# Memory cross-attention of a two-layer decoder trunk: queries made transposed in two half blocks, heads taken in pairs

## The chip, the core and the metric

The kernel runs on one core of a Trainium2 chip. The metric is the device time of one launch in microseconds (us), as a median of several runs. Six engines appear below: PE (TensorE) multiplies matrices into the accumulation memory PSUM, DVE (VectorE) and ACT (ScalarE) do elementwise work, POOL (GpSimd) here does one elementwise job only, SP (SyncE) issues the transfers of the weights. Each engine runs its own instructions in the order in which the code issues them, and waits on semaphores for the others.

## What is computed

Two layers, each with three sub-layers that add to the rows `x` (256 tokens, 1024 columns). The change is in the second sub-layer:

```
def memory_xattn(h, mem_h, wq, wk, wv, q_norm, k_norm, wo):
    q = rms_norm((h @ wq).reshape(B, S, XA_HEADS, XA_HEAD_DIM), q_norm)
    k = rms_norm((mem_h @ wk).reshape(B, M, XA_HEADS, XA_HEAD_DIM), k_norm)
    v = (mem_h @ wv).reshape(B, M, XA_HEADS, XA_HEAD_DIM)
    s = jnp.einsum('bshd,bmhd->bhsm', q, k).astype(jnp.float32) * (XA_HEAD_DIM ** -0.5)
    p = jax.nn.softmax(s, axis=-1)
    o = jnp.einsum('bhsm,bmhd->bshd', p.astype(v.dtype), v).reshape(B, S, XA_WIDTH)
    return o @ wo
...
x = x + merged @ w_out[l]
x = x + memory_xattn(rms_norm(x, xa_norm[l]), rms_norm(mem, mem_norm[l]), ...)
x = x + peer_ffn(rms_norm(x, ffn_norm[l]), ...)
```

There are 4 heads of 128, 256 tokens and 256 memory rows. `rms_norm` divides a row by the root of its mean square. Around this sub-layer stand the output projection of the first one (`w_out`) and the expert network, which takes most of the time and is not touched.

## The kernel before

**Weights come as a stream of pieces.** A piece is 128 x 512 numbers of some weight matrix. The table `ORDER` lists the pieces of a layer: the blocks out0, out1 (`w_out`), xq (8 pieces of `wq`), xo0, xo1 (4 pieces each of `wo`, by halves of the output columns), pq0, pq1 (8 each, queries of the expert network), and before and behind them other blocks. For each piece ACT rounds it to a high part (`hi`, L495), POOL subtracts that to get the low part (L464), and PE multiplies with both. There are four slots for pieces, so ACT and POOL work on a piece only when PE is done with the piece four places ahead of it (semaphore `used`). On PE, `take(n)` (L853) takes the next n pieces. A normal piece is six matmuls with 512 moving columns (L874 to L876): the activations are held stationary and the weights move. A piece of pq0 or pq1 (`query_piece`, L843) is twelve matmuls with 256 moving columns (L848 to L850): here the weights are stationary, and the result comes out transposed.

**Order of the work.** There is no scheduler: each engine's order is the order of the code. PE around the change is at L1036 to L1100, ACT at L644 to L696, DVE at L1573 to L1646. `rows_T` transposes rows through PE; `hi_T` on ACT and `lo_T` on DVE then make the high and low parts of the transposed rows that the next pieces multiply. `a.step` and `d.step` make ACT and DVE wait for each of their own instructions before the next.

**The attention.** PE takes all 8 xq pieces, the last 6 of them in one go (L1039). DVE scales the queries by the rows' norm (L1589), ACT squares them (L659), DVE sums the squares (L1593), PE transposes the queries (L1045, recorded at L824), ACT copies them with the gain (L662), ACT takes the root (L551) and switches its function table to exp (L665). Then come four units, each of one 128-token half and one pair of heads: scores on PE (`xscores`, L1051), maximum on DVE (L1605, L1606), exp on ACT with the sum on the side (L669), transposition of the probabilities on PE (`xprobs`, recorded at L824), copy on DVE (L1611), values on PE (`xvalues`, L1068). At the end of each token half DVE divides by the sums (L1621, L1623), PE transposes the result (L1088), `hi_T` and `lo_T` split it, and PE goes on with `take(6)` (L1092): the four pieces of xo0 and the first two of xo1. Then it waits until DVE has added xo0 to X (`add_block`, L1571), transposes the first half of X (L1096), and takes four more pieces.

No piece of the weight stream is multiplied between the last xq piece and the first xo piece.

## Time and profile before

| | us |
|---|---|
| median of 3 runs | 2165.35 (2164.05 to 2165.48) |
| the profiled execution | 2163.49 |
| its span, first to last instruction | 2161.7 |
| PE busy / POOL busy / DVE busy / ACT busy | 2124.3 / 1716.0 / 1244.7 / 1191.0 |

The profiled execution is 1.86 us below the median of the runs; 1.79 us of it lie outside the span. The granted TensorE clock is full over the whole span. Times in the trace are microseconds from the first instruction. The two layers are the same code in a loop: what stands at 259 us in the first layer stands again at 1330 us in the second, with gaps of the same length, so the text reads the first layer and doubles.

### The profile page before, as it was taken

The page shows a single profiled execution, that of the slowest core. Times are in us where ns is not written, and L with a number is a line of the kernel's source. Part 1 is how long each engine was busy: PE and PEld are TensorE (multiplying, and loading weights), DVE is VectorE, ACT ScalarE, POOL GpSimd, SP SyncE. Part 2 cuts the span into 40 slices and gives each one's busy share as a digit, 9 for nine tenths or more (in the row PEclk, how much of TensorE's full clock was granted, in tenths as well). Part 3 has the DMA queues.
Part 4 walks back from the last instruction along what each step waited for, and adds up shares of the span by engine and source line. Part 5 has one row for each costly group of instructions (what it writes and reads, how often), then busy time and mean ns, then how long its engine had stood idle before and what let it go on. Part 6 is the DMA issues. An engine that isn't in the chain of part 4 may idle for free.

```text
span 2161.7 us, 50003 instructions
## 1 busy us (share of the span) xinstructions
PE 2124.3 (98%) x14654; PEld 1832.6 (85%) x14654; DVE 1244.7 (58%) x2401; ACT 1191.0 (55%) x2285; POOL 1716.0 (79%) x1316
## 2 busy tenths in 40 slices
PE   7999999999999999999999999999999999999999
PEld 6777799999888888888877777999988888888887
DVE  6655548876666655433347564489666665554334
ACT  5455765555555545556555556655555555545565
POOL 6766768988888888888887676798888888888887
PEclk9999999999999999999999999999999999999999
DMA  7433435555455555565574343455555444545555
GB/s 273 156 129 120 162 132 171 181 180 169 162 167 163 166 167 169 175 204 188 192 247 139 127 136 127 157 176 184 175 171 168 161 166 163 171 165 195 189 190 175
DMA packets 100825, 367.92 MB, mean 170 GB/s; under 512 B 11520, under 2 KB 12032, under 8 KB 100480
## 3 DMA queue, kind: packets, MB, share of 16 engines
q1 hardware_dynamic: 97344, 354.46, 49.2%
q10 hardware_dynamic: 3392, 12.35, 1.5%
q8 instruction: 46, 0.75, 0.2%
q14 instruction: 43, 0.35, 0.0%
HBM read 365.72 MB, written 1.05 MB: 170 GB/s over the span
## 4 chain that ended last, share of the span: by engine, by line
PE 95%; issue 2%; ACT 1%; DVE 1%; POOL 1%; POOLq 0%; ACTq 0%; DVEq 0%
PE acc L1116 11%; PE acc L1201 11%; PE acc L1203 11%; PE acc L1202 11%; PE acc L874 6%; PE acc L876 6%; PE acc L875 6%; PE acc L1106 5%; PE acc L1107 5%; PE acc L1108 5%; PE acc L1115 5%; PE aux L1160 4%; PE aux L824 2%; PE aux L981 1%; PE aux L1014 1%
## 5 line engine op out<-in xcount | busy, mean ns | idle before, releaser
L464 POOL TENSOR_TENSOR w_lo<-raw,w_hi 128x512 fp32r<-128x512 f32 x1312 | 1715.8, 1319 | 436.1 <-ACT w_hi L495 318.3
L495 ACT ACTIVATE w_hi<-raw 128x512 fp32r<-128x512 f32 x1348 | 844.1, 629 | 679.5 <-PE acc L876 186.3
L1201 PE MATMUL acc<-w_hi,eg 128*128 128x512 f32 x1024 | 406.2, 397 | 0.0
L1203 PE MATMUL acc<-w_hi,eg 128*128 128x512 f32 x1024 | 399.6, 390 | 0.0
L1202 PE MATMUL acc<-w_lo,eg 128*128 128x512 f32 x1024 | 398.7, 389 | 0.0
L1116 PE MATMUL acc<-h_rows,w_hi 128*128 128x512 f32 x1024 | 362.5, 398 | 0.0
L1775 DVE TENSOR_TENSOR eg<-big,eg 128x256 fp32r<-128x256 f32 x256 | 172.8, 675 | 235.6 <-ACT eg L716 229.3
L1106 PE MATMUL acc<-h_rows,w_hi 128*128 128x256 f32 x1024 | 290.6, 284 | 1.1 <-POOL w_lo L464 1.1
L1107 PE MATMUL acc<-h_rows,w_hi 128*128 128x256 f32 x1024 | 289.8, 283 | 0.0
L1108 PE MATMUL acc<-h_rows,w_lo 128*128 128x256 f32 x1024 | 289.7, 283 | 0.0
L1115 PE MATMUL acc<-h_rows,w_lo 128*128 128x256 f32 x896 | 249.5, 278 | 0.0
L1203 PEld LDWEIGHTS acc<-w_hi,eg 128*128 128x128 f32 x1024 | 192.2, 188 | 41.5
L1202 PEld LDWEIGHTS acc<-w_lo,eg 128*128 128x128 f32 x1024 | 192.6, 188 | 38.3
L1201 PEld LDWEIGHTS acc<-w_hi,eg 128*128 128x128 f32 x1024 | 192.4, 188 | 38.4 <-issue 0.6
L716 ACT ACTIVATE eg<-big 128x256 fp32r (+1 forms) x256 | 106.8, 418 | 204.1 <-PE acc L1203 204.1
L1116 PEld LDWEIGHTS acc<-h_rows,w_hi 128*128 128x128 f32 x1024 | 187.7, 188 | 32.9
L1106 PEld LDWEIGHTS acc<-h_rows,w_hi 128*128 128x128 f32 x1024 | 196.5, 192 | 2.0 <-POOL w_lo L464 1.6
L1107 PEld LDWEIGHTS acc<-h_rows,w_hi 128*128 128x128 f32 x1024 | 196.6, 192 | 0.0
L1108 PEld LDWEIGHTS acc<-h_rows,w_lo 128*128 128x128 f32 x1024 | 196.6, 192 | 0.0
L1732 DVE TENSOR_TENSOR hot_b<-aux,sel 128x1024 bf16<-128x1024 bf16 x128 | 88.6, 692 | 154.7 <-PE aux L1160 145.8
L1115 PEld LDWEIGHTS acc<-h_rows,w_lo 128*128 128x128 f32 x896 | 168.6, 188 | 5.7
L874 PE MATMUL acc<-w_hi,h_rows 128*128 128x512 f32 x384 | 159.7, 416 | 10.1 <-POOL w_lo L464 3.3
(251 smaller groups left out, 2926.4 us busy)
## 6 DMA issues: line engine op xcount, KB each, us to landing
raw<-stream_dram SPq DMA_DIRECT2D x674, 512.0 KB, 3.3
big<-parb_dram ACTq DMA_DIRECT2D x2, 2128.0 KB, 10.2
big<-mem_dram ACTq DMA_DIRECT2D x3, 1024.0 KB, 5.3
big<-pm_dram ACTq DMA_DIRECT2D x2, 768.0 KB, 15.2
X<-x_dram ACTq DMA_DIRECT2D x1, 1024.0 KB, 7.0
out_dram<-X SPq DMA_DIRECT2D x2, 512.0 KB, 2.9
big<-parr_dram ACTq DMA_DIRECT2D x2, 448.0 KB, 11.9
big<-lnrow_dram ACTq DMA_DIRECT2D x2, 256.0 KB, 12.9
```

Source lines behind the costliest of these rows:

```text
L464: nc.gpsimd.tensor_tensor(w_lo[:, k % SLOTS, :], raw[:, k // PER_CHUNK, k % PER_CHUNK, :], w_hi[:, k % SLOTS, :].bitcast(F32), ALU.subtrac ...
L495: nc.scalar.activation(w_hi[:, k % SLOTS, :], raw[:, (k // PER_CHUNK) % RAW, k % PER_CHUNK, :], ACT.Copy).then_inc(hi_ready, 1)
L874: pe_.matmul(dst, r_hi[:, kt, ts], w_hi[:, slot, :], start=first, stop=False)
L1106: pe_.matmul(dst, wh, h_hi[:, kt, :], start=(kt == 0), stop=False)
L1107: pe_.matmul(dst, wh, h_lo[:, kt, :], start=False, stop=False)
L1108: return pe_.matmul(dst, w_lo[:, r % SLOTS, wk * P:(wk + 1) * P], h_hi[:, kt, :], start=False, stop=(kt == KD - 1))
L1115: pe_.matmul(acc[:, bank_of, 0:S], w_lo[:, r % SLOTS, at], h_hi[:, kt, :], start=False, stop=False)
L1116: ins = pe_.matmul(acc[:, bank_of, :], w_hi[:, r % SLOTS, at], h_rows[:, kt, :, :], start=(kt == 0), stop=(kt == KD - 1))
L1201: pe_.matmul(dst, eg[:, q % 2, 0, ts], w_hi[:, slot, :], start=start, stop=False)
L1202: pe_.matmul(dst, eg[:, q % 2, 0, ts], w_lo[:, slot, :], start=False, stop=False)
L1203: ins = pe_.matmul(dst, eg[:, q % 2, 1, ts], w_hi[:, slot, :], start=False, stop=stop)
L1775: V.tensor_tensor(eg[:, q % 2, 1, :], src, eg[:, q % 2, 0, :].bitcast(F32), ALU.subtract).then_inc(sig["eg_ready"].sem, 1)
```

## The change

- The xq block is laid out and multiplied another way. Its pieces are now for one pair of heads and 256 rows of the weight; the weights are stationary and the queries come out transposed, in twelve matmuls with 256 moving columns (`x_query_piece`). The order of the pieces is 0, 1, 4, 5, 2, 3, 6, 7, so the first pair's queries are there two pieces before the end of the block. The transposition of the queries (8 PE transposes and their copies) is gone.
- The norm of the input rows is no longer applied to the queries. Sums of squares of each head are made on PE by multiplying the squares with a column of ones (`xsum`, four matmuls with one moving column), and the root takes the rows' norm in as its bias. For the first pair ACT takes the root; for the second pair DVE computes the inverse root by shifts and three Newton steps (`inverse_root`, twelve small instructions). The query gain goes into the keys (`mkT`).
- The units are ordered by head pair, first both token halves of pair 0, then of pair 1. The probabilities are scaled by the inverse sums on DVE before they are transposed (`x_scale`); the values are stationary, so the result comes out transposed and goes to `hi_T` and `lo_T` without further transposes. ACT copies the transposed probabilities of units 0 and 1, DVE those of units 2 and 3.
- The order of the xo pieces is now xo0 0, xo0 1, xo1 0, xo1 1, xo0 2, xo0 3, xo1 2, xo1 3. PE takes the last xq piece between the scores, and the first three xo pieces around the second pair's probabilities.

```
+_at = ORDER.index(("xq", 0))
+ORDER[_at:_at + KD] = [("xq", k) for k in (0, 1, 4, 5, 2, 3, 6, 7)]
+_at = ORDER.index(("xo0", 0))
+ORDER[_at:_at + KD] = [(b, 2 * half + k) for half in range(2) for b in ("xo0", "xo1") for k in range(2)]
```

On ACT:

```
+                a.step(nc.scalar.activation(st[:, 96:97], ident[:, 0:1], ACT.Sqrt))
...
+                x_square(0)
+                hi(2)
+                a.wait("x_mean", 2)
+                a.wait("xq_sums", 1)
+                for t in range(T):
+                    a.step(nc.scalar.activation(xr[:, 2 * t:2 * t + 2], xsums[:, 0, 2 * t:2 * t + 2], ACT.Sqrt, bias=ssx[:, t:t + 1]),
+                           "xq_sqrt" if t else None)
+                a.step(nc.scalar.activation(st[:, 96:97], ident[:, 0:1], ACT.Exp))
+                x_exps(0)
+                x_exps(1)
+                x_square(1)
+                x_probs(0)
+                hi(1)
+                x_probs(1)
+                hi_T("xo_T0", 0, 2)
+                x_exps(2)
+                hi(1)
+                x_exps(3)
+                hi(2)
+                hi_T("xo_T1", 2, 2)
+                hi(3)
```

On PE:

```
+                xsum(0)
+                e.wait("xq_rows", 1)
                 e.wait_block("mem_v")
+                xscores(0)
+                xscores(1)
+                take(1)
+                e.wait_block("xq")
+                xscores(2)
                 xprobs(0)
+                xscores(3)
+                xsum(1)
+                xprobs(1)
+                xvalues(0)
+                xvalues(1)
+                take(2)
+                xprobs(2)
+                take(1)
+                xprobs(3)
+                xvalues(2)
+                xvalues(3)
+                take(3)
```

On DVE:

```
+                def x_scale(u):
                     t, j = XUNITS[u]
+                    d.wait_drained(f"xs{u}")
+                    d.step(V.reciprocal(coef[:, 2 * u:2 * u + 2], sums[:, t, 2 * j:2 * j + 2]))
+                    for h in range(2):
+                        d.step(V.tensor_scalar(xring[:, u, h, :], xring[:, u, h, :], coef[:, 2 * u + h:2 * u + h + 1], None, ALU.mult),
+                               "xp_scaled" if h else None)
...
+                x_queries(0)
+                d.wait("xq_sqrt")
+                d.step(V.reciprocal(xr[:, 0:4], xr[:, 0:4]))
+                for u in range(2):
+                    x_top(u)
+                    x_bias(u)
+                x_queries(1)
+                x_scale(0)
+                x_scale(1)
+                x_top(2)
+                x_top(3)
...
+                inverse_root(xr[:, 4:8], xarg, xtmp)
+                x_bias(2)
+                x_bias(3)
+                lo_T("xo_T0", 0, 2)
+                x_scale(2)
+                x_probs(2)
+                x_scale(3)
+                x_probs(3)
+                lo_T("xo_T1", 2, 2)
```

On PE, behind the xq pieces. Before, the values of a unit (L1068) are followed by the transposes of the result (L1088) and then the first xo piece (L874):

```order
1250 L1068 MATMUL aux<-big 128x128 [waits aux3_drained]
1251 L1068 MATMUL aux<-big 128x128 x3
1252 L1088 MATMUL aux<-cst,big 128x128 [waits xo_ready,aux3_drained,aux1_drained]
1253 L1088 MATMUL aux<-cst,big 128x128 x3
1254 L1088 MATMUL aux<-cst,big 128x128 [waits xo_ready]
1255 L1088 MATMUL aux<-cst,big 128x128 x3
```

Now the second pair's units stand between pieces. L858 are the transposes of the probabilities (they wait for `xp_scaled`, DVE's scaling), L922 begins a piece, L1118 are the values:

```order
1306 L387 REGISTER_ALU [waits xp_scaled]
1307 L858 MATMUL aux<-cst,big 128x128 [waits aux2_drained]
1308 L858 MATMUL aux<-cst,big 128x128 x3
1309 L909 REGISTER_ALU [waits acc_free0]
1310 L922 MATMUL acc<-w_hi,h_rows 128x512 [waits lo_ready]
...
1317 L858 MATMUL aux<-cst,big 128x128 [waits aux0_drained,xp_scaled]
1318 L858 MATMUL aux<-cst,big 128x128 x3
1319 L382 REGISTER_ALU
1320 L1118 MATMUL aux<-big 128x128 [waits aux1_drained,aux2_drained]
```

What moved: the transposes of the result are gone, and three pieces have come in between the units.

On ACT, around the exps of the last two units. Before (L669 is the exp, L539 `hi_T`) no piece is prepared among them:

```order
506 L669 ACTIVATE big,st<-aux,st 128x256 [waits act_step]
507 L373 REGISTER_ALU
508 L363 REGISTER_ALU [waits aux2_drained]
509 L669 ACTIVATE big,st<-aux,st 128x256 [waits xs_ready]
510 L669 ACTIVATE big,st<-aux,st 128x256 [waits act_step]
```

Now (L677 is the exp, L504 the preparation of a piece, which waits for PE's `used`):

```order
508 L677 ACTIVATE big,st<-aux,st 128x256 [waits act_step]
509 L382 REGISTER_ALU
510 L503 REGISTER_ALU [waits chunk_in2,aux2_drained]
511 L504 ACTIVATE w_hi<-raw 128x512 [waits used]
512 L372 REGISTER_ALU
513 L677 ACTIVATE big,st<-aux,st 128x256 [waits xs_ready]
514 L677 ACTIVATE big,st<-aux,st 128x256 [waits act_step]
```

What moved: the exp of the last unit now stands behind a piece's preparation, which waits for the first xo piece to be multiplied.

On DVE, the end of the attention. Before, the division (L1623) reads PSUM and is followed by `lo_T` (L1267):

```order
384 L1621 RECIPROCAL st<-st 128x4 [waits aux0_drained,aux3_drained]
385 L1623 TENSOR_TENSOR big<-aux,st 128x512 [waits aux2_filled,dve_step]
386 L373 REGISTER_ALU
387 L363 REGISTER_ALU [waits aux2_drained]
388 L1267 SCALAR_TENSOR_TENSOR h_rows<-aux,h_rows 128x256 [waits hi_T]
```

Now the scaling (L1660) reads and writes the on-chip buffer `big`, twice per unit:

```order
374 L1667 COPY big<-aux 128x512 [waits aux2_filled,xp_scaled]
375 L382 REGISTER_ALU
376 L382 REGISTER_ALU [waits aux2_drained]
377 L1658 RECIPROCAL st<-st 128x2 [waits aux0_drained]
378 L1660 TENSOR_SCALAR big<-big,st 128x256 [waits dve_step] x2
379 L1667 COPY big<-aux 128x512 [waits aux0_filled,xp_scaled]
```

What moved: the scaling stands ahead of the transposition of the probabilities, in the chain of each unit, and no longer once behind the values.

## Rows read from the trace of the kernel before

**Rows 1.** The page: busy time of the engines; the chain that ended last, by engine.

```profile
PE 2124.3 (98%) x14654; PEld 1832.6 (85%) x14654; DVE 1244.7 (58%) x2401; ACT 1191.0 (55%) x2285; POOL 1716.0 (79%) x1316
...
PE 95%; issue 2%; ACT 1%; DVE 1%; POOL 1%; POOLq 0%; ACTq 0%; DVEq 0%
```

**Rows 2.** Busy time in three windows: length, then PE, PEld, DVE, ACT, POOL.

```profile
249.86:259.12 9.26, 9.26 (x45) 7.35 (x43) 2.99 (x7) 8.06 (x16) 8.09 (x8) 1.00 0.40 135
259.12:276.32 17.20, 12.32 (x80) 10.10 (x80) 12.38 (x25) 11.77 (x29) 3.40 (x3) 1.00 0.22 82
276.32:284.64 8.32, 8.32 (x36) 6.82 (x37) 2.22 (x4) 3.16 (x5) 5.63 (x5) 1.00 0.20 65
```

**Rows 3.** PE's timeline, first layer: start, length, instruction group, idle time and releaser.

```profile
258.73 0.39 PE L876 MATMUL acc<-w_hi,h_rows 128*128 128x512 f32 x1
262.30 3.69 PE L1051 MATMUL aux<-big 128*128 128x256 f32 x16 [0.90 <-ACT big L662]
266.23 0.63 PE L824 MATMUL aux<-cst,big 128*128 128x128 f32 x4 [0.24 <-ACT big L669]
269.14 0.63 PE L824 MATMUL aux<-cst,big 128*128 128x128 f32 x4
269.61 1.06 PE L1068 MATMUL aux<-big 128*128 128x128 f32 x8
270.60 0.63 PE L824 MATMUL aux<-cst,big 128*128 128x128 f32 x4
276.32 0.50 PE L874 MATMUL acc<-w_hi,h_rows 128*128 128x512 f32 x1 [1.59 <-DVE h_rows L1267]
```

**Rows 4.** PE's timeline where the first half of X is transposed.

```profile
284.64 1.04 PE L824 MATMUL aux<-cst,X 128*128 128x128 f32 x8
```

**Rows 5.** PE's timeline: a small projection; a piece with 256 moving columns and what follows.

```profile
101.15 0.58 PE L942 MATMUL aux<-cst,big 128*128 128x24 f32 x4
101.57 0.48 PE L874 MATMUL acc<-w_hi,eg 128*128 128x512 f32 x1
...
288.25 0.28 PE L848 MATMUL acc<-eg,w_hi 128*128 128x256 f32 x1
291.10 1.03 PE L824 MATMUL aux<-cst,X 128*128 128x128 f32 x8
```

**Rows 6.** ACT's timeline around the attention: table load, root, square, exp, `hi_T`, next piece.

```profile
256.47 1.28 ACT L551 ACT_TABLE_LOAD   x1
257.77 0.20 ACT L551 ACTIVATE st<-st 128x2 f32<-128x2 f32 x1
259.94 0.63 ACT L659 ACTIVATE big<-big 128x512 f32<-128x512 f32 x1 [0.16 <-DVE big L1589]
264.75 0.56 ACT L669 ACTIVATE big<-aux,st 128x256 f32<-128x256 f32 x1
266.20 0.56 ACT L669 ACTIVATE big<-aux,st 128x256 f32<-128x256 f32 x1
274.55 1.71 ACT L539 ACTIVATE h_rows<-aux 128x256 fp32r<-128x256 f32 x4 [4.10 <-PE aux L1088]
278.02 0.63 ACT L495 ACTIVATE w_hi<-raw 128x512 fp32r<-128x512 f32 x1 [1.76 <-PE acc L876]
```

**Rows 7.** DVE's timeline: a copy from PSUM, `lo_T` behind the attention, xo0 added.

```profile
269.81 0.69 DVE L1611 COPY big<-aux 128x512 f32<-128x512 f32 x1 [0.57 <-PE aux L824]
275.38 1.89 DVE L1267 SCALAR_TENSOR_TENSOR h_rows<-aux,h_rows 128x256 fp32r<-128x256 f32 x4 [1.42 <-ACT h_rows L539]
282.12 1.41 DVE L1571 TENSOR_TENSOR X<-X,acc 128x512 f32<-128x512 f32 x2 [4.84 <-PE acc L876]
```

**Rows 8.** Single lines of DVE: durations in ns, smallest, median, largest.

```profile
L1580 DVE TENSOR_TENSOR st<-st x4: 714/717/720, 255.2 to 1367.5; 128x2 f32<-128x2 f32 x4
L1606 DVE TENSOR_TENSOR st<-st x8: 160/161/161, 264.5 to 1339.5; 128x2 f32<-128x2 f32 x8
L1293 DVE TENSOR_SCALAR big<-X,st x8: 753/862/1660, 25.6 to 1371.5; 128x1024 f32<-128x1024 f32 x8
L1389 DVE TENSOR_TENSOR big<-big,st x8: 436/1398/1401, 84.1 to 1158.6; 128x256 f32<-128x256 f32 x8
L1418 DVE TENSOR_SCALAR big<-big,st x4: 414/414/414, 98.7 to 1172.1; 128x256 f32<-128x256 f32 x4
```

**Rows 9.** POOL's timeline: the low parts of the pieces.

```profile
253.38 5.26 POOL L464 TENSOR_TENSOR w_lo<-raw,w_hi 128x512 fp32r<-128x512 f32 x4 [0.89 <-ACT w_hi L495]
278.72 8.12 POOL L464 TENSOR_TENSOR w_lo<-raw,w_hi 128x512 fp32r<-128x512 f32 x6 [16.20 <-ACT w_hi L495]
```

**Rows 10.** DVE's timeline: two small sums right behind each other while POOL works.

```profile
255.23 0.72 DVE L1580 TENSOR_TENSOR st<-st 128x2 f32<-128x2 f32 x1 [1.59 <-ACT big L545]
255.98 0.17 DVE L1288 TENSOR_SCALAR st<-st 128x2 f32<-128x2 f32 x1
```

More of the change, by code:

```diff
@@ L46 @@
 LOWEST = -3.0e38
+ROOT_SCALE = 6.245058920000258e+18
 PER_CHUNK = 2
@@ L258, in trunk @@
         zg_fold = cst[:, K_ZF:K_ZF + 24]
+        ones = cst[:, K_ON:K_ON + 1]
         rows1 = region("rows1", 2048)
@@ L684, in _ @@
                     hi((3, 2)[n])
-                root(ssx, "x_mean", "x_sqrt", 3)
+                a.wait("x_mean", 3)
+                a.step(nc.scalar.activation(ssx, ssx, ACT.Sqrt), "x_sqrt")
                 hi(3)
@@ L1038, in _, with xsum @@
                     rows_T([f"xa_T{i}" for i in (2 * n, 2 * n + 1)], X, 4 * n)
[L1039 to L1045 removed]
+                    take((4, 5)[n])
+                def xsum(j):
+                    e.wait("xq_square", j + 1)
+                    for t in range(T):
+                        for h in range(2):
+                            ins = pe_.matmul(xsums[:, j, 2 * t + h:2 * t + h + 1], xsquare[:, j, h * S + t * P:h * S + (t + 1) * P], ones,
+                                             start=True, stop=True)
+                    ins.then_inc(sig["xq_sums"].sem, 1)
                 def xscores(u):
```

187 lines of the change are left out of this document (81 added, 106 removed).

## The prediction

> **What bounds the kernel now.** I read the page first: PE is busy for 98% of the span and is 95% of the chain that ended last [rows 1]. So a change pays only where PE waits or works on something else than pieces. Then the windows around the attention: in the 9.26 us before the last xq piece ends, and again in the 8.32 us behind the first xo piece's start, PE is busy throughout; between them lie 17.20 us in which it is busy for 12.32 and multiplies no piece, while POOL has 3.40 us of work [rows 2]. PE's timeline shows what fills them: transposes and small matmuls with waits for ACT and DVE between, the last 1.59 us for `lo_T` [rows 3]. That is the stretch the change rebuilds. I follow one layer on PE up to the start of the transposes of X, at 284.64 us [rows 4]. Behind them every engine has the same work in both kernels (on PE the seventh and eighth xo piece, then pq0), so what shifts that start shifts the end, twice, once per layer. From the last xq piece's end to there PE needs today 17.20 + 8.32 = 25.5 us.
>
> **Up to the last xq pieces.** A piece with 512 moving columns takes 8.32/6 = 1.39 us [rows 2]; two pieces with 256 columns take 291.10 − 288.25 = 2.85, so 1.43 each [rows 5]. The eight xq pieces thus cost 8 x 0.04 = 0.3 us more, of which the first seven lie ahead of the point where PE now leaves them: about 258.0 us, where the seventh is done. PE then waits for the squares of pair 0: ACT loads the table for the root (1.28) and takes a dummy root (0.20) from 256.5 on, so to 258.1, and squares for 0.63 [rows 6]; with a hand-over of 0.1 PE goes on at 258.9, after **0.9** us idle.
>
> **The sums on PE.** A matmul with one moving column is not in the trace. The nearest row is the 24-column one: 4 recorded passes in 101.57 − 101.15 = 0.42 [rows 5], 0.105 each; from above, a 128-column pass, 1.06 for 8, 0.13 [rows 3]. Four matmuls are 8 passes: 0.84 to 1.06, I take **0.95**, twice per layer, because the 24-column row is the nearest and the first pass has to start up. They replace the 8 transposes of the queries.
>
> **The first pair.** One unit's scores take 3.69/4 = 0.92, four transposes 0.46 (269.61 − 269.14), values 0.99 (270.60 − 269.61) [rows 3]. Scores 0 and 1 end at 261.7, the last xq piece at 263.2. Scores 2 wait for DVE's copy of the second pair's queries (0.69 [rows 7], with hand-overs to 264.2): **1.0** idle. Then scores 2, transposes 0, scores 3, sums 1, transposes 1, values 0 and 1: 0.92 + 0.46 + 0.92 + 0.95 + 0.46 + 1.98 = 5.7, to 269.95. The exps of one unit take 1.45 (266.20 − 264.75) [rows 6] and keep pace: exp 0 from 262.4, exp 1 to 265.2, scale of unit 1 to 266.2.
>
> **The second pair's root and the first xo piece.** `hi_T` for two rows is 1.71/2 = 0.85 [rows 6], `lo_T` 1.89/2 = 0.95 [rows 7]: the xo piece could start at 269.95 + 0.1 + 0.85 + 0.95 = 271.85. DVE gets to `lo_T` only after the inverse root. Its sums are there at 267.8; then come one addition, twelve instructions on 4 columns and two biases, each like the 0.16 of a 2-column product [rows 8] plus 0.04 to the next: 15 x 0.2 = 3.0, so 270.8, just in time. With POOL in the way (below) it is 271.6 and the piece starts at 272.5. I take **272.5**, since POOL gets the fourth xo piece at 267.5 and works on it for 1.3. Today this piece starts at 276.32 [rows 3]: a lead of 3.8 us (4.5 at best).
>
> **From there to the transposes of X.** Today six pieces back to back, 8.3 us. Now, from the first xo piece's start t:
> - two pieces to t + 2.9; transposes 2 and the third piece to t + 4.9.
> - Meanwhile ACT can only prepare the fifth xo piece when the first is done, and today it does that 278.02 − 276.32 = 1.70 after the start [rows 3, 6]. The exp of unit 3 stands behind it: 1.70 + 0.54 + 1.34, done at t + 3.6. DVE copies unit 2 to t + 4.25, then scales unit 3: reciprocal 0.2 and two multiplies of 128 x 256 from buffer to buffer. A multiply has 0.75 for 1024 columns as its smallest row and 0.41 for 256 in a form with two scalars [rows 8]; between 0.3 and 0.41 I take 0.35. Unit 3 is scaled at t + 5.25, and PE has waited 0.4.
> - transposes 3, values 2 and 3: to t + 7.8. The fourth piece runs beside `hi_T` (0.85) and the fifth waits for `lo_T` (0.95): it starts at t + 9.7, after **0.5** idle. Fifth and sixth piece to t + 12.6.
> - The sixth is the last piece of xo0. DVE adds xo0 in 1.41 [rows 7]; today two more pieces of xo1 run over that (the addition starts at 282.12, the transposes at 284.64). In the new order nothing does: the four pieces `take` brings behind the wait are the ones that used to cover it. **1.5** to 1.6 us idle, to t + 14.2.
>
> With t = 272.5 that is 286.7, **2.1 us later** than today; with t = 271.85 it is 286.05, 1.4 later.
>
> **POOL and DVE at the same memory.** DVE instructions that read or write only the on-chip buffer wait while POOL works. A sum of 2 columns takes 0.72 at 255.23 us, under POOL's run from 253.38 to 258.64, and the same kind takes 0.16 in the attention, where POOL idles [rows 8 to 10]. Four products of 128 x 256 in a row take 0.436 once and then 1.40 each [rows 8]; 1024-column multiplies run from 0.75 to 1.66. POOL's instruction is 5.26/4 = 1.3 long [rows 9], and a DVE instruction caught by it waits for its end. Reading PSUM is not hit, so today's attention is nearly free of it: POOL idles for 16.20 us and DVE reads PSUM. The GPSIMD Engine Reference of the Trainium skill (Key points) says the same: the two share their buffer interfaces, with contention for DVE instructions with two buffer inputs or in a two-port mode. Its page VectorE: DVE Perf Modes (Mode 2×_2P) puts a 32-bit multiply by a scalar from buffer to buffer in that mode. By both the new scaling is hit, and the trace agrees, in the 0.75 to 1.66 of the 1024-column multiplies; if the rule didn't hold for it, the sum would be the 2.1 above.
>
> The scaling of unit 3 meets POOL almost exactly. ACT prepares the sixth xo piece right behind the exps, from t + 3.7 to t + 4.33, and POOL starts at t + 4.4; the first multiply is due at t + 4.5. If the multiply gets in first, or is only just caught, one multiply waits for one POOL instruction: +1.2. If both are caught, the first by the sixth piece and the second by the seventh (ready at t + 5.75), it is +2.5. PE waits for both.
>
> I choose **one** block: 2.1 + 1.2 = 3.3 us per layer, 6.6 in all. The profiled execution would be 2163.5 + 6.6 = 2170.1; the median lies 1.86 above it, 2165.35 + 6.6 = **2172.0**.
>
> **The rivals.**
> 1. Both multiplies are caught, as three of four products at L1389 are [rows 8]: 2.1 + 2.5 = 4.6 per layer, 9.2, 2174.6 us. For it speaks that POOL is 0.1 ahead; against it that one hand-over off by 0.1 undoes it.
> 2. Not slower by more than can be told: no multiply is caught, since they are short and come between POOL's instructions, as one of 2 columns does in 0.17 at 255.98, right behind one that was caught [rows 10]. Then 1.4 to 2.1 per layer, 2168.2 to 2169.6. It decides at whether the multiply starts before t + 4.4. To lose less than that, the end of xo0 would have to be covered, and its place in the order is fixed.
> 3. The hand-overs hide as the order seems to mean: PE waits neither 0.9 for the squares, nor 1.0 for the copy, nor the 0.9 behind the third and fourth piece. That takes 2.8 off t + 14.2: −0.7 to −1.4 per layer, 2163 to 2164; it would need ACT's table load and DVE's copy to end a microsecond earlier. With also the addition covered (−1.5) it is 4 to 6 us faster, 2160. Only this one is faster by more than can be told.
>
> That the change fails to do what it says is hardly open, since every engine's order is written out; what is open is only whether the pieces moved in between save anything, and that is the sum above.
>
> **How the numbers follow.** Less than 0.2%, 4.3 us, can't be told from no change. Forecast 0.38; both caught 0.23; none caught 0.23; hidden hand-overs without gain 0.09; faster 0.07. The forecast's own spread, mostly the start t (271.85 to 272.7) and the multiply (0.3 to 0.41), is ±1.5 in all, so it lies in slower with nearly all of its chance; of "none caught" about a quarter reaches past 4.3. That makes slower 0.67, same 0.25, faster 0.08. The range goes from 2166.5 (below the best case of rival 2, into rival 3) to 2175.5 (rival 1 with its spread).
>
> **What would show it.** Right: no piece-free stretch over 5 us; the first xo piece starts 3.5 to 4.5 earlier relative to the end of the xq block's seventh piece than the sum of today's parts; PE waits about 1.5 for X's addition right behind the sixth xo piece, and about 1.0 for the copy of the second pair's queries; one of the scaling multiplies of unit 3 takes over 1 us. Wrong: the piece start of xo later than 273 or earlier than 271.5 at the first layer; a sum of squares on PE over 1.2; scaling rows that stay at 0.35 while POOL works; or new waits behind the transposes of X, which I hold to be the same.

## The result, and the profile after

The changed kernel takes 2172.06 us (median of 6 runs, 2171.46 to 2175.69), beside 2165.41 us for the kernel before on the same chip (6 runs, 2164.05 to 2165.79): 6.65 us slower, ratio 1.0033 with a 95% interval of 1.0022 to 1.0043. The forecast was 6.6 us. The sum behind it holds in most of its terms and not in all, and the next sections take it apart. Two executions far above all others, one of 2328.09 us in run 11 and one of 5487.9 us of the kernel before beside runs 9 to 11, are left out of the ranges and ratios below.

The page of the changed kernel, the same two lines as [rows 1]: busy time of the engines, and the chain that ended last.

```profile
PE 2129.0 (98%) x14750; PEld 1840.5 (85%) x14750; DVE 1245.7 (57%) x2429; ACT 1191.9 (55%) x2287; POOL 1716.3 (79%) x1316
...
PE 93%; issue 2%; DVE 2%; ACT 2%; POOL 1%; POOLq 0%; ACTq 0%; DVEq 0%
```

PE is still the bound, but its share of the chain is down from 95% to 93%: it waits more. This execution took 2173.24 us with a span of 2171.4, 9.7 more than the 2161.7 of before's. The two marks that bound the attention on PE say where the 9.7 lie. They are the starts of the transposes of X, first ahead of the xq block and then behind the attention (lines 858; they were 824 before, and 284.64 in [rows 4] is the second of them):

| | ahead of xq | behind the attention | between | before's |
|---|---|---|---|---|
| layer 1 | 244.50 | 289.63 | 45.13 | 41.15 |
| layer 2 | 1319.25 | 1365.44 | 46.19 | 41.15 |

So 3.98 and 5.04 us come from inside, one layer each. Of the rest, 1.0 was lost before the first mark (244.50 for 243.49); in the thirteen profiles of this document that mark stands anywhere from 243.33 to 246.04, so this is no price of the change that one profile could show. And the stretches between the layers (1029.6 for 1030.0) and behind the second (806.0 for 805.9) are the same as before. Two of the six executions, with spans of 2169.7, are 8.0 above before's span, which is 2 x 3.98.

PE's timeline through the first layer's attention, as [rows 3] showed it for the kernel before (start, length, instruction group, in brackets the idle time ahead of it and what ended it):

```profile
259.85 1.05 PE L1093 MATMUL acc<-cst,big 128*128 128x1 f32 x8 [0.62 <-ACT big L669]
260.76 1.97 PE L1101 MATMUL aux<-big 128*128 128x256 f32 x8
...
264.94 1.13 PE L1101 MATMUL aux<-big 128*128 128x256 f32 x4 [0.78 <-DVE big L1641]
...
268.64 2.01 PE L1118 MATMUL aux<-big 128*128 128x128 f32 x16
273.36 0.50 PE L922 MATMUL acc<-w_hi,h_rows 128*128 128x512 f32 x1 [2.71 <-DVE h_rows L1318]
...
276.23 0.60 PE L858 MATMUL aux<-cst,big 128*128 128x128 f32 x4
...
280.49 0.66 PE L858 MATMUL aux<-cst,big 128*128 128x128 f32 x4 [2.27 <-DVE big L1660]
...
285.13 0.47 PE L922 MATMUL acc<-w_hi,h_rows 128*128 128x512 f32 x1 [0.57 <-DVE h_rows L1318]
...
289.63 1.09 PE L858 MATMUL aux<-cst,X 128*128 128x128 f32 x8 [1.50 <-DVE X L1623]
```

Six waits stand there, 8.45 us together: for the squares of pair 0, for the copy of pair 1's queries, for `lo_T` ahead of the first xo piece, for the scaling of unit 3, for `lo_T` of the second pair, and for the addition to X. The first xo piece starts 28.86 behind the first mark (before: 276.32 − 243.49 = 32.83), so 3.97 are won up to there; from it to the second mark there are 16.27 us instead of 8.32 [rows 2].

DVE's timeline in the same stretch. Line 1671 is the first step of the inverse root, 1660 the two multiplies that scale a unit (of unit 2 at 273.81, of unit 3 at 277.95):

```profile
268.99 0.83 DVE L1671 TENSOR_SCALAR st<-st 128x4 uint32<-128x4 uint32 x1
269.86 0.17 DVE L1672 TENSOR_SCALAR st<-st 128x4 uint32<-128x4 uint32 x1
...
273.81 0.74 DVE L1660 TENSOR_SCALAR big<-big,st 128x256 f32<-128x256 f32 x2
...
277.95 2.48 DVE L1660 TENSOR_SCALAR big<-big,st 128x256 f32<-128x256 f32 x2
```

POOL's timeline beside it:

```profile
268.53 1.27 POOL L473 TENSOR_TENSOR w_lo<-raw,w_hi 128x512 fp32r<-128x512 f32 x1 [5.42 <-ACT w_hi L504]
...
277.74 2.54 POOL L473 TENSOR_TENSOR w_lo<-raw,w_hi 128x512 fp32r<-128x512 f32 x2 [0.69 <-ACT w_hi L504]
```

With POOL idle two multiplies take 0.74; under POOL's two instructions both are caught, which means that each ends only behind the POOL instruction that runs beside it, and they take 2.48. All of this line's instructions, in ns (smallest, median, largest): a free multiply is 0.352 us, a caught one 1.233.

```profile
L1660 DVE TENSOR_SCALAR big<-big,st x16: 352/353/1233, 265.2 to 1355.9; 128x256 f32<-128x256 f32 x16
```

The second layer differs, and it brings something that the forecast had not: TensorE's granted clock. PE's timeline there, with the first matmuls of the first xo piece:

```profile
1348.11 0.80 PE L922 MATMUL acc<-w_hi,h_rows 128*128 128x512 f32 x1 [2.70 <-DVE h_rows L1318]
1348.70 0.63 PE L923 MATMUL acc<-w_lo,h_rows 128*128 128x512 f32 x1
...
1353.39 0.98 PE L858 MATMUL aux<-cst,big 128*128 128x128 f32 x4
...
1356.30 0.66 PE L858 MATMUL aux<-cst,big 128*128 128x128 f32 x4 [0.54 <-DVE big L1660]
```

The same in windows of 5 us (length, then PE, PEld, DVE, ACT, POOL; the last three columns are the granted clock, the DMA share and GB/s):

```profile
1340.00:1345.00 5.00, 5.00 (x38) 4.52 (x37) 4.25 (x11) 3.43 (x8) 1.26 (x1) 1.00 0.01 3
1345.00:1350.00 5.00, 2.30 (x9) 1.72 (x8) 3.50 (x16) 2.08 (x6) 0.00 (x0) 0.73 0.32 105
1350.00:1355.00 5.00, 5.00 (x17) 3.99 (x16) 0.52 (x1) 2.46 (x6) 1.94 (x2) 0.58 0.00 0
```

Inside PE's wait of 2.70 us the granted clock falls from 2.4 to 1.2 GHz, and stays there for 6.8 us. The two pieces and the transposes behind them take 5.28 and 0.71 us, where the first layer took 2.87 and 0.35: 2.8 us lost. In return ACT and POOL come at other times. DVE's timeline with the scaling of unit 3, then POOL's:

```profile
1355.50 0.74 DVE L1660 TENSOR_SCALAR big<-big,st 128x256 f32<-128x256 f32 x2
```

```profile
1354.34 1.30 POOL L473 TENSOR_TENSOR w_lo<-raw,w_hi 128x512 fp32r<-128x512 f32 x1 [1.28 <-ACT w_hi L504]
1356.51 1.26 POOL L473 TENSOR_TENSOR w_lo<-raw,w_hi 128x512 fp32r<-128x512 f32 x1 [0.87 <-ACT w_hi L504]
```

The scaling starts 0.14 before one POOL instruction ends and is over before the next begins. It takes its free 0.74, and PE waits 0.54 for it instead of 2.27. 3.98 + 2.8 − 1.73 is the second layer's 5.04, to 0.01.

The text on the kernel before said that its clock is full over the whole span. That holds for both attentions and not for the span: behind a wait of 2.42 us that ends at 21.32, its trace has 3.4 us at half clock (mean granted clock 0.67 from 20 to 25 us).

### The profile page after: what moved, and what is told of

The parts are those of the page before. It is cut to its first block, busy times and chain, and to the rows that moved or that the text cites. A ratio compares the mean times of both kernels' runs of the same rounds, so it can differ in the third digit from the quotient of the medians.

```text
span 2171.4 us, 50185 instructions
## 1 busy us (share of the span) xinstructions
PE 2129.0 (98%) x14750; PEld 1840.5 (85%) x14750; DVE 1245.7 (57%) x2429; ACT 1191.9 (55%) x2287; POOL 1716.3 (79%) x1316
## 4 chain that ended last, share of the span: by engine, by line
PE 93%; issue 2%; DVE 2%; ACT 2%; POOL 1%; POOLq 0%; ACTq 0%; DVEq 0%
PE acc L1167 11%; PE acc L1252 11%; PE acc L1254 11%; PE acc L1253 11%; PE acc L922 6%; PE acc L924 5%; PE acc L923 5%; PE acc L1157 5%; PE acc L1158 5%; PE acc L1159 5%; PE acc L1166 5%; PE aux L1211 4%; PE aux L858 2%; PE aux L1029 1%; POOL w_lo L473 1%
## 5 line engine op out<-in xcount | busy, mean ns | idle before, releaser
L504 ACT ACTIVATE w_hi<-raw 128x512 fp32r<-128x512 f32 x1348 | 844.4, 629 | 682.6 <-PE acc L924 187.5
L1840 DVE TENSOR_REDUCE big<-acc 128x512 f32 (+1 forms) x128 | 88.5, 691 | 139.4 <-PE acc L1167 135.8
```

Source lines behind the costliest of these rows:

```text
L504: nc.scalar.activation(w_hi[:, k % SLOTS, :], raw[:, (k // PER_CHUNK) % RAW, k % PER_CHUNK, :], ACT.Copy).then_inc(hi_ready, 1)
```

## The experiments

All kernels leave nothing out, and each is timed beside the kernel before on the same chip. Four were run together (median of before 2164.36), then four on another chip (2164.65), then three on the chip of the first four (2165.43). The changed kernel itself stands 6.65 us over before in the result and 8.6 in run 5, so medians of different groups that differ by less than 2 us show nothing; there the traces have to decide. "Marks" are the two starts of X's transposes as above; before has 41.15 us between them in either layer.

**1. The order of the xo block alone.** The kernel before, with only the new order of the xo pieces:

```diff
+_at = ORDER.index(("xo0", 0))
+ORDER[_at:_at + KD] = [(b, 2 * half + k) for half in range(2) for b in ("xo0", "xo1") for k in range(2)]
 PROJ = len(ORDER)
```

> The kernel before with one part of the change alone: the xo pieces in the new order (xo0 0, xo0 1, xo1 0, xo1 1, xo0 2, xo0 3, xo1 2, xo1 3). Theory (the addition of xo0 to X loses its cover): the last xo0 piece is now the sixth, right ahead of the transposes of X, so TensorE waits 1.5 us there per layer and nothing else moves: 3.0 us over the kernel before. Rival (the cost of that place comes from the other edits): the same time as before, within 0.7 us.

Measured: 2168.38 us (2166.86 to 2171.04), ratio 1.0018 (1.0009 to 1.0027), so 4.0 over before. PE's timeline, the transposes of X behind the attention in both layers:

```profile
288.90 1.09 PE L826 MATMUL aux<-cst,X 128*128 128x128 f32 x8 [1.58 <-DVE X L1573]
...
1362.21 1.09 PE L826 MATMUL aux<-cst,X 128*128 128x128 f32 x8 [1.58 <-DVE X L1573]
```

The wait that the order uncovers is there as forecast, and the marks lie 42.86 apart in both layers, 1.71 more than before. It costs 3.4 us between the marks on its own (expected: 3.0), about half of the whole change's loss.

**2. The addition covered again.** The changed kernel, with the seventh xo piece (of xo1) ahead of the transposes of X:

```diff
-                take(3)
+                take(4)
...
-                    take((4, 7)[n])
+                    take((3, 7)[n])
```

> The changed kernel with the seventh xo piece taken ahead of the transposes of X instead of behind them. Theory: the 1.5 us wait for the addition falls to about 0.1, but only one piece is left to hide the splitting of the transposed rows (2.2 us) from the first pq0 piece, a new wait of 0.8 to 0.9: 0.6 less per layer, 1.2 us below the changed kernel. Rival: the wait only moves to the pq0 piece in full, no difference.

Measured: 2171.30 us (2170.90 to 2175.88), ratio 1.0036 (1.0023 to 1.005). The wait of 1.50 for X is gone in both layers. What came instead stands one piece later, in front of pq0, in PE's timeline:

```profile
291.82 0.39 PE L882 MATMUL acc<-eg,w_hi 128*128 128x256 f32 x1 [0.36 <-DVE h_lo L1318]
```

So 1.1 us a layer should be won (1.50 − 0.36), twice the 0.6 of the expectation, which had put the new wait at 0.8 to 0.9. The median is 0.8 under the changed kernel's 2172.06, but against before it is 6.9 over, where the changed kernel was 6.65 over, and both layers of this profile have a stretch of 3.4 us at half clock. The wait moved as the theory said; that it is worth anything in time this run doesn't show.

**3. POOL kept away from the scaling.** On ACT alone, the two w_hi steps behind the exps of unit 3 go behind `hi_T` of the second pair:

```diff
                 x_exps(3)
-                hi(2)
                 hi_T("xo_T1", 2, 2)
-                hi(3)
+                hi(5)
```

> The changed kernel with ScalarE preparing the sixth and seventh xo piece behind the splitting of the second pair's result instead of ahead of it, so that GpSimd is idle while VectorE scales the probabilities of unit 3. Theory (two multiplies are caught by GpSimd): both multiplies at that place take 0.35 us each in both layers, the wait of TensorE for them falls from 2.3 to about 0.5, 1.2 to 1.8 us less per layer where they were caught, 2.4 to 3.5 us in all. Rival (the prepared pieces come too late then, or TensorE is bound by something else there): less than 0.7 us difference, and a new wait for GpSimd ahead of the sixth or seventh piece.

Measured: 2170.98 us (2170.04 to 2172.34), ratio 1.003 (1.0019 to 1.0042). PE's wait for the scaling of unit 3, both layers:

```profile
278.50 0.66 PE L857 MATMUL aux<-cst,big 128*128 128x128 f32 x4 [0.53 <-DVE big L1659]
...
1353.10 0.66 PE L857 MATMUL aux<-cst,big 128*128 128x128 f32 x4 [0.52 <-DVE big L1659]
```

With POOL idle there (its next run starts at 282.89) no multiply is caught, and no new wait for POOL appears. The wait falls from 2.27 to 0.53 and the first layer's marks from 45.13 to 43.44. That prices both catches together at 1.7 us. In the second layer the changed kernel had no catch to lose (0.54), and both have low-clock stretches there, so only one layer's 1.7 was to be had there: the expectation of 2.4 to 3.5 counted it in both. The median is 1.1 under the changed kernel's, but the distance from before is the same (6.6 for 6.65): the gain is shown in the trace, not in the time.

**4. The second pair in one go.** The interleaving undone: xo in its old order, all six pieces behind the second pair, no w_hi step among the second pair's exps. On PE:

```diff
-                take(2)
                 xprobs(2)
-                take(1)
                 xprobs(3)
                 xvalues(2)
                 xvalues(3)
-                take(3)
+                take(6)
```

> The changed kernel with the interleaving of the second pair undone: no xo piece between its units, all six behind them in the old order, and ScalarE prepares no piece among its exps. Theory: the lead of 4 us is given up, but the exp of unit 3 no longer stands behind a piece, no multiply is caught, and the addition of xo0 is covered by two pieces again: transposes of X 2.2 us later than in the kernel before per layer, 4.4 us over it, 2.2 below the changed kernel. Rival (interleaving pays, and only the caught multiplies cost): slower than the changed kernel by 1 us or more.

Measured: 2173.86 us (2172.38 to 2174.68), ratio 1.0042 (1.0028 to 1.0055). It was expected 2.2 below the changed kernel and is not below it; that it is slower isn't shown either, since the intervals overlap and the profiled spans are 2171.5 and 2171.4. PE's timeline of the first layer:

```profile
273.50 1.11 PE L854 MATMUL aux<-cst,big 128*128 128x128 f32 x4 [4.02 <-DVE big L1654]
276.53 1.11 PE L854 MATMUL aux<-cst,big 128*128 128x128 f32 x4 [1.92 <-DVE big L1654]
277.44 3.62 PE L1114 MATMUL aux<-big 128*128 128x128 f32 x16
```

Its windows of 5 us, columns as above:

```profile
270.00:275.00 5.00, 1.11 (x4) 0.71 (x4) 3.00 (x13) 3.00 (x9) 0.00 (x0) 0.74 0.25 93
275.00:280.00 5.00, 3.47 (x17) 3.47 (x17) 1.98 (x5) 0.00 (x0) 0.00 (x0) 0.50 0.01 3
280.00:285.00 5.00, 5.00 (x20) 4.20 (x20) 0.85 (x2) 1.77 (x4) 1.03 (x1) 0.74 0.00 0
```

The pieces between the units had kept PE at work. Without them it waits 4.02 and 1.92 us, and the granted clock is at half for 10.2 us in each layer: the values of two units take 3.62, where they take 2.01 at full clock. The marks lie 46.55 and 46.13 apart. That the clock falls because PE waits was at this point a guess from the order of events; runs 5 to 7 and run 9 test it.

**5. The same kernel again.** The changed kernel, beside the next three.

> The changed kernel, unchanged, on the same chip as the next three, so that they are compared with it and not with a run elsewhere. Both theories expect 2171.5 to 2173 us as median, some 7 us over the kernel before. It also shows whether the stretches in which TensorE's clock is granted at half come and go from run to run: in the one profile of it so far the first layer's pieces behind PE's wait of 2.71 us ran at full clock, the second layer's at half for 6.83 us.

Measured: 2173.24 us (2172.65 to 2175.78), ratio 1.0042 (1.0028 to 1.0056). That is 8.6 over before, a little above the expected range of 2171.5 to 2173. In its profile both layers have a stretch of 3.4 us at half clock: in the first layer behind the wait of 2.25 for the scaling (at 281), in the second behind the 2.72 ahead of the first xo piece (at 1349). So where it strikes, and whether, changes from one execution to the next.

**6. PE kept at work in one wait.** The changed kernel with extra transposes of a constant:

```diff
                 xvalues(1)
+                for _ in range(18):
+                    pe_.transpose(bank("xo_T1")[:, 0:P], ident, ident)
                 take(2)
```

> The changed kernel with 18 extra transposes of a constant in PE's wait of 2.71 us ahead of the first xo piece (18 x 0.115 = 2.1 us of work where PE had none; nothing else is changed, and nothing is left out). Theory: it is the idle PE that lets the granted clock fall there. Then neither layer has a stretch at half clock around the attention, the wait shrinks to about 0.6, the first xo piece starts as before (28.9 behind the first transposes for the xq block), and the median falls by 0.7 to 1.5 us against the changed kernel on this chip, with a smaller spread. Rival: the clock falls for another reason (or by chance), the profile shows a half-clock stretch all the same, and the median is the same within 0.4.

Measured: 2172.05 us (2171.41 to 2172.67), ratio 1.0033 (1.002 to 1.0045), 1.2 below the run beside it and with less spread (1.3 us for 3.1). PE's timeline of the first layer:

```profile
272.27 0.50 PE L922 MATMUL acc<-w_hi,h_rows 128*128 128x512 f32 x1 [0.75 <-DVE h_rows L1320]
...
279.40 1.11 PE L858 MATMUL aux<-cst,big 128*128 128x128 f32 x4 [2.27 <-DVE big L1662]
280.30 3.17 PE L1118 MATMUL aux<-big 128*128 128x128 f32 x16
```

Behind the filled wait the clock stays up in both layers, and the first xo piece starts 28.87 behind the first mark, as expected. It falls at the other one, 2.27 for the scaling, in the first layer (values 3.17 for 2.17) and not in the second. The expectation had forgotten that wait, so "no stretch around the attention" was wrong; that no fall follows the filled wait agrees with the theory, but two layers alone could be chance, since the unfilled wait had no fall in some layers either.

**7. Both waits of run 4 filled.** The clean test: 28 extra transposes in the wait of 4.02, 12 in that of 1.92.

```diff
                 xvalues(1)
+                for _ in range(28):
+                    pe_.transpose(bank("xo_T1")[:, 0:P], ident, ident)
                 xprobs(2)
+                for _ in range(12):
+                    pe_.transpose(bank("xo_T1")[:, 0:P], ident, ident)
                 xprobs(3)
```

> The kernel labelled together (second pair in one go, all six xo pieces behind it) with 28 and 12 extra transposes in PE's two waits of 4.02 and 1.92 us. In together both layers ran at half clock for 10.24 us there; its values took 3.62 where 2.01 is the full-clock time, its transposes 1.11 for 0.63, its first xo pieces had 0.43 between matmuls for 0.23, which adds up to 4.5 to 5 us per layer. Theory (the clock fell because of the waits): no half-clock stretch, and 9 to 10 us less than together, so 2164 to 2165.5, about the kernel before. Rival (the waits for the scaled probabilities are the loss, and the clock is a side effect that costs little): at most 3 us less, 2171 or more.

Measured: 2170.28 us (2167.76 to 2171.95), ratio 1.0026 (1.0015 to 1.0036). PE's timeline, first layer:

```profile
274.85 0.65 PE L854 MATMUL aux<-cst,big 128*128 128x128 f32 x4 [0.96 <-DVE big L1658]
275.34 1.47 PE L1137 MATMUL aux<-cst 128*128 128x128 f32 x12
277.42 0.66 PE L854 MATMUL aux<-cst,big 128*128 128x128 f32 x4 [0.61 <-DVE big L1658]
277.91 2.17 PE L1114 MATMUL aux<-big 128*128 128x128 f32 x16
```

More work for PE, and the kernel is 3.6 us faster than run 4 (3.9 by the distances from before). No window of either layer's attention is below full clock, and the marks are 43.46 and 43.45 apart, 3.1 and 2.7 less than in run 4. In the code only PE's extra work differs from run 4, so this is the strongest evidence that PE's idleness lets the clock fall and that work without any use holds it. The count over all profiles agrees. Behind the values of unit 1, where the extra transposes go, the changed order and its versions have a wait of 1.94 to 4.03 us in 14 layers, and 8 of them have a fall there; in the 8 layers where that wait was filled (runs 6, 7, 9 and 11) there is none. The size was overrated: the time lies between the theory's 9 to 10 us and the rival's 3 at most. I had expected 9 to 10 us, but the useful work waits for DVE at the same times in both kernels (the 28 transposes and the 0.96 behind them take the place of the 4.02), and only what runs behind the waits gets faster. By its marks it also shows that run 4's own expectation, 4.4 over before, was right but for the clock: 2 x 2.3 us; its median is 5.6 over.

**8. A version with the waits taken out.** From what runs 1 to 4 showed, the changed kernel with four moves. ACT:

```diff
                 x_probs(0)
-                hi(1)
                 x_probs(1)
                 hi_T("xo_T0", 0, 2)
-                x_exps(2)
                 hi(1)
+                x_exps(2)
                 x_exps(3)
                 hi(2)
                 hi_T("xo_T1", 2, 2)
-                hi(3)
+                hi(4)
```

DVE, `x_scale(3)` ahead of `x_probs(2)`; and PE:

```diff
                 take(2)
                 xprobs(2)
-                take(1)
                 xprobs(3)
                 xvalues(2)
                 xvalues(3)
-                take(3)
+                take(5)
...
-                    take((4, 7)[n])
+                    take((3, 7)[n])
```

> The changed kernel with four things moved, nothing left out: ACT takes the fourth xo piece behind hi_T of xo_T0 instead of between the two copies of probabilities (so that GpSimd doesn't work during the inverse root), and both exps of the second pair back to back; DVE scales unit 3 before it copies unit 2; PE takes two xo pieces, then the whole second pair, then five pieces, one of them the seventh, which covers the addition to X. Worked out from the rows of the changed kernel: first xo piece 0.6 to 0.9 earlier (no catch of 0.66 in the root), no wait for the scaling (2.27 and 0.54), 0.3 for the copy of unit 2, no wait for lo_T (0.65), no wait for X's addition (1.50) but 0.36 ahead of pq0. From the first transposes for the xq block to those of X 41.3 us with one more xo piece of 1.40 done by then. Theory: 2163 to 2165.5 us, 7 to 9 below the changed kernel, at or just below the kernel before. Rival: the clock falls in PE's remaining wait of 2.0 us and costs 1.5 to 3.4 per layer: 2166.5 to 2169.

Measured: 2164.81 us (2163.04 to 2167.40, 11 runs), ratio 1.0 (0.9991 to 1.0009): 8.4 below the changed kernel beside it, and equal to the kernel before. PE's timeline, first layer, then the first xo piece of the second:

```profile
271.97 0.50 PE L921 MATMUL acc<-w_hi,h_rows 128*128 128x512 f32 x1 [1.99 <-DVE h_rows L1316]
...
276.29 2.05 PE L1117 MATMUL aux<-big 128*128 128x128 f32 x16 [0.28 <-DVE big L1665]
...
285.29 1.09 PE L857 MATMUL aux<-cst,X 128*128 128x128 f32 x8
288.14 0.39 PE L881 MATMUL acc<-eg,w_hi 128*128 128x256 f32 x1 [0.36 <-DVE h_lo L1316]
...
1342.83 0.60 PE L921 MATMUL acc<-w_hi,h_rows 128*128 128x512 f32 x1 [2.00 <-DVE h_rows L1316]
```

The waits of 2.27, 0.57 and 1.50 are gone for 0.28 and 0.36, and the inverse root is no longer caught (its first step takes 0.17). The marks are 41.52 apart in the first layer with one more piece done between them. In the second layer they are 43.14 apart: there the clock was at half for 3.4 us behind the wait of 2.00. So the mechanism of the rival came, in one layer of two, and the median is still in the theory's range.

**9. The same, with the last long wait filled** by 14 extra transposes behind `xvalues(1)`, as in run 6.

> The kernel labelled best with 14 extra transposes of a constant (14 x 0.115 = 1.6 us) in PE's remaining wait of 2.0 us ahead of the first xo piece. In best's profile the second layer ran at half clock for 3.41 us behind that wait, the first did not. Theory (idle PE lets the clock fall): no half-clock stretch in either layer, X's transposes 41.5 behind those of the xq block in both layers instead of 41.52 and 43.14, median 2162.5 to 2164.5 and a smaller spread than best's 2163.0 to 2167.4. Rival (chance): as best, 2164.8 within 0.4, spread unchanged.

Measured: 2164.23 us (2162.50 to 2167.15, 11 runs), ratio 0.9997 (0.9988 to 1.0007). The profile has no stretch at half clock in either layer, and the marks lie 41.56 apart in both. The span is 2160.7, 2.3 less than in run 8. The medians of the two differ by 0.6 and the spread did not shrink: the clock's part is seen in the trace, and no gain is shown in the time.

**10. The squares earlier.** Run 8, with ACT's table load for the root and the squares of pair 0 one w_hi step earlier:

```diff
                     half_squares(n)
-                    hi((3, 2)[n])
+                    hi((3, 1)[n])
...
                 x_square(0)
-                hi(2)
+                hi(3)
```

> The kernel labelled best with ACT's load of the table for the root, the dummy root and the squares of pair 0 taken one w_hi step earlier (0.55 us), that step now behind the squares. Theory: PE's wait of 0.62 for the squares goes, since the queries' copy is done 0.14 before ACT would start the squares then, and everything behind moves 0.3 to 0.6 earlier, as ACT's roots come 0.3 earlier: 0.6 to 1.2 us off the median of best, 2163.6 to 2164.2. Rival: GpSimd's three steps in a row now catch DVE's product for the bias of unit 0 (0.16 free, up to 0.83 caught, as with the root's first step in the changed kernel), the exps of unit 0 start no earlier, and nothing is gained or up to 1 us lost: 2164.8 to 2166.

Measured: 2165.75 us (2164.14 to 2168.20, 11 runs), ratio 1.0007 (0.9998 to 1.0016): no gain, as the rival has it. The wait of 0.62 for the squares is gone and the one for the copy has grown from 0.78 to 1.17; the marks are 41.36 and 42.97 apart, 0.16 and 0.17 less than in run 8. PE's timeline:

```profile
263.98 1.13 PE L1100 MATMUL aux<-big 128*128 128x256 f32 x4 [1.17 <-DVE big L1639]
```

DVE's timeline, where POOL catches the bias of unit 1 (0.41 for 0.16), not that of unit 0 as the rival said, just ahead of that copy:

```profile
262.70 0.41 DVE L1650 TENSOR_TENSOR st<-st 128x2 f32<-128x2 f32 x1
263.24 0.69 DVE L1639 COPY big<-acc 128x512 f32<-128x512 f32 x1
```

**11. Also the copy's wait covered,** by the scores of unit 1 behind the last xq piece, with run 10's step and 12 extra transposes:

```diff
                 xscores(0)
-                xscores(1)
                 take(1)
+                xscores(1)
                 e.wait_block("xq")
                 xscores(2)
-                xprobs(0)
                 xscores(3)
+                xprobs(0)
                 xsum(1)
```

> best_early, and besides: PE takes the last xq piece between the scores of units 0 and 1 and does the scores of units 2 and 3 in a row, ACT squares pair 1 between the exps of units 0 and 1, DVE's order follows, and 12 extra transposes of a constant lie in the wait ahead of the first xo piece. Theory: the piece's wait of 0.78 for the copy of the second pair's queries is covered by the scores of unit 1 (0.92), and the first xo piece comes 0.5 us earlier than in best_early; with that and no half-clock stretch 2161 to 2163, below the kernel before by 0.1%. Rival: DVE is the bound from the copy to lo_T (busy without a gap), the gap only moves to the wait ahead of the first xo piece, and the time is best_fill's less what best_early gains.

Measured: 2164.11 us (2162.27 to 2166.35), ratio 0.9998 (0.9988 to 1.0007), as run 9 and above the 2161 to 2163 of the theory. The wait for the copy is gone (0.78 and 1.17 before), one of 0.65 for the scaling of unit 1 has come, and the first xo piece starts 27.96 behind the first mark, where run 10 has 28.02 and run 9 has 28.19: 0.06 earlier than in run 10, and not the 0.5 of the theory. The marks are 41.27 and 41.32 apart, 0.3 less than in run 9. PE's waits up to the first xo piece are DVE's work seen from the other side: DVE is busy nearly without a gap from the copy of pair 1's queries to `lo_T`, and closing one wait opens the next.

No version is faster than the kernel before by more than its interval.

## Why the prediction was right, and where it was not

The total was right: forecast 2172.0, measured 2172.06, in the range of 2166.5 to 2175.5. Point by point, against the first layer of the changed kernel's trace:

| step | forecast | measured |
|---|---|---|
| wait for the squares of pair 0 | 0.9 | 0.62 |
| sums of squares on PE, each | 0.95 | 0.91, 0.81 |
| wait for the copy of pair 1's queries | 1.0 | 0.78 |
| first xo piece, behind the first mark | 29.0 | 28.86 |
| wait for `lo_T` ahead of the first xo piece | 2.55 (269.95 to 272.5) | 2.71 |
| one multiply of the scaling, free | 0.35 | 0.352 |
| what one catch adds to it | 1.2 | 0.88 (1.233 − 0.352) |
| wait for the scaling of unit 3 | 1.6 (0.4 + 1.2) | 2.27; 0.54 in layer 2 |
| wait for `lo_T` of the second pair | 0.5 | 0.57 |
| wait for the addition to X | 1.5 | 1.50 |
| cost per layer | 3.3 | 3.98; 5.04 in layer 2 |

The sums are from start to start (259.85 to 260.76, 267.37 to 268.18). The lead of the first xo piece, 3.97, was forecast at 3.8, and the inverse root was caught once by POOL as taken (0.83 for 0.17). The last wait is confirmed by itself in runs 1 and 2.

**The step that failed is the term for caught multiplies, in its number and in its price.** The forecast took one catch at 1.2, in both layers. The first layer has both (the case of rival 1), the second none (that of rival 2), so the two halves of the forecast's middle lie on either side of it. A catch adds 1.233 − 0.352 = 0.88 and not 1.2; the prediction's own row, 1.40 for 0.436, would have said 0.96. Run 3 gets 1.7 back for both catches, which is 2 x 0.88, where the prediction's rival had 2.5. So the first layer's wait of 2.27 is the 0.53 of run 3 and two catches, instead of 0.4 + 1.2: too few catches at too high a price, and the two errors cancel in part.

The number of catches did not hang on a tenth, as the prediction had it; it went with the clock. The changed kernel, run 2 and run 6 leave this part of the order alone. In all five of their layers in which the two pieces ahead of the scaling ran at full clock (changed, layer 1; again, layer 1; run 2, layer 2; run 6, both), the scaling begins 0.20 to 0.23 behind POOL and takes 2.47 to 2.49: both are caught. In the three with a half-clock stretch ahead of it, it takes 0.74 (the 6.8 us stretch) and 1.02 (the two of 3.4 us). That the 0.352 and 1.233 stand on one and the same line agrees with the Trainium skill (GPSIMD Engine Reference, Key points), which states contention between the two engines at the buffer interfaces that they share, for a VectorE instruction in a two-port mode or with two buffer inputs.

**What the forecast lacked is the clock.** Its rivals listed waits and catches only; a wait was counted at its own length. In the second layer 2.8 us are lost because the work behind the wait ran at 1.2 GHz, more than any single term of the sum but the lead. None of the signs that it named for "wrong" covers this.

**Two of its signs were badly put.** "No piece-free stretch over 5 us" contradicts the prediction's own sum, which has the last xq piece end at 263.2 and the first xo piece start at 272.5; the trace has 264.16 to 273.36, 9.2 us. And 273.36 is later than the 273 that it named as a sign of being wrong, but 1.0 of it lies before the first mark: measured from there, the start came 0.15 early.

**So the total is partly luck.** At full clock the trace says 2 x 3.98 = 8.0, 1.4 above the forecast, or 0.7 a layer, which is what the wait for the scaling is above its 1.6; with half-clock stretches it is more. Timed again in run 5, the changed kernel was 8.6 over before, not 6.65. The medians differ by less than the best spans do, since before's median lies 1.9 us above the execution that was profiled and the changed kernel's lies 0.6 above its best. Why before's own executions spread by 2 us stays open. Its one profile shows no half-clock stretch in the attention, but one of 3.4 us behind the wait that ends at 21.32, and none behind a wait of 2.39 that ends at 13.11, where the profiles of runs 2, 5, 6 and 7 do show such a stretch. If these come and go as in the attention, they are a likely source; no run tests it.

Rival 3, hidden hand-overs, has nothing for it in the changed kernel, as all three of its waits are there. Runs 8 to 11 show what it would take: four moves on three engines bring the loss to zero, and the further ones bring no gain that can be told from zero.

## What to carry to other kernels

Moving matmul pieces in between dependent small steps wins only if what they used to cover stays covered: here the order of the xo block was the price, 1.7 us a layer, and that could be read beforehand from which addition ends the wait behind the last piece. A wait of PE has to be counted at its length plus what runs slowly behind it; waits like the ones of 1.94 to 4.03 us here are worth filling with a useful piece. Useless work in them kept the clock up too; in time it gained 3.6 us in run 7 and 1.2 in run 6, and nothing that could be told from zero in run 9. And when DVE gets a new instruction with only buffer operands, look at what POOL does in that microsecond: the 128x256 multiply here took from 0.35 to 1.23 us by that alone.

## What the runs showed of the hardware

TensorE's granted clock falls to half in waits of 2 to 4 us, or shortly behind them. I looked at both layers' attention in all thirteen profiles, 26 layers. In the ten whose longest PE wait there is 1.59 us or less (before, runs 1, 7, 9 and 11) no window of 1 us is below full clock. In the sixteen with a wait of 1.94 us or more, eleven have a stretch at half clock, beginning in such a wait or up to 1.3 us behind it:

| kernel | longest waits, us | stretch at half clock, us (layer 1; layer 2) |
|---|---|---|
| changed | 2.71, 2.27; 2.70 | none; 6.8 |
| changed, again | 2.71, 2.25; 2.72 | 3.4; 3.4 |
| run 2 | 2.71; 2.71, 2.27 | 3.4; 3.4 |
| run 3 | 2.70; 2.71 | none; 3.4 |
| run 4 | 4.02, 1.92; 4.03, 1.92 | 10.2; 10.2 |
| run 6 | 2.27; 2.27 | 3.4; none |
| run 8 | 1.99; 2.00 | none; 3.4 |
| run 10 | 1.94; 1.94 | none; 3.4 |

The price, read from rows at both levels: 2.8 us for the 6.8 of the changed kernel, 1.6 (43.14 − 41.52) for the 3.4 of run 8, 3.1 and 2.7 for the 10.2 of run 4. The same wait sometimes brings the fall and sometimes not, and it moves the marks of run 8 by 1.6 us, so it is a likely source of the spread from run to run. What decides it these runs don't show. The Trainium skill (TensorE: Matmul & The Clock Gate, HAM oscillation) tells of the same thing between bursts of matmuls that wait for DMA; the runs agree with it in kind.

Second, a DVE instruction of 4 columns is caught by POOL as well as a large one: the first step of the inverse root took 0.83 for 0.17, from 268.99 to 269.82, and POOL's instruction beside it ended at 269.80. A copy from PSUM beside POOL kept its 0.69 (at 257.83).
